# One of the modulation chunks leaves the attention loop of a one-core diffusion step and is weighed by VectorE during the output projection

## The chip, the cores and the metric

The kernel runs on one core of one Trainium2 chip. The metric is the device time of one launch in microseconds; lower is better. All data is float32 except a few small routing tables.

## What is computed

Two layers of a diffusion backbone over 384 tokens (128 context, 256 latent) of width 1024. Layer 0 mixes by a short convolution and an eight-head latent attention, layer 1 by a chunked gMLP. Each layer then runs a mixture of 16 experts. Every mixer and every mixture is shifted, scaled and gated by six vectors of 1024 that come from the condition:

```python
    for l in range(DEPTH):
        mp = jnp.split((jax.nn.silu(c_ctx) @ w_ada[l] + b_ada[l])[None, None, :], 6, axis=-1)
        ms = jnp.split((jax.nn.silu(c) @ w_ada[l] + b_ada[l])[:, None, :], 6, axis=-1)
        hp = modulate(rmsnorm(xp, g_mix[l]), mp[0], mp[1])
        hs = modulate(rmsnorm(xs, g_mix[l]), ms[0], ms[1])
        ...
        xp = xp + mp[2] * op
        xs = xs + ms[2] * os_
        hp = modulate(rmsnorm(xp, g_ffn[l]), mp[3], mp[4])
        hs = modulate(rmsnorm(xs, g_ffn[l]), ms[3], ms[4])
        xp = xp + mp[5] * moe(hp, router_w, router_b, moe_w1[l], moe_w3[l], moe_w2[l])
        xs = xs + ms[5] * moe(hs, router_w, router_b, moe_w1[l], moe_w3[l], moe_w2[l])
```

The change is about one product of this kind, `silu(c) @ w_ada`.

## The kernel before

**The modulation chunks.** The product with `w_ada` (1024 x 12288 over both layers) is cut into 16 chunks "ada 0" to "ada 15" of 768 columns and 3 MB each; four chunks make the vectors of one half-layer. A chunk goes through four steps. `ada_rows(n)` on TensorE multiplies the weights by the two condition vectors: 48 matmuls of 128 columns, which the trace counts as 96 records. ScalarE copies the result to `ada_row`. `ada_turned(n)` on TensorE transposes it. `ada(n)` on VectorE adds the bias into `mod` in three instructions; for every n with n % 4 == 2 a fourth computes `gain1`.

Two chunks, `WEIGHED = (3, 4)`, are done another way. VectorE multiplies each of the eight 128x768 weight tiles by the condition values and adds them up, once for each of the two condition vectors (`weigh`, 16 instructions). TensorE then only sums over the partitions (`weighed_rows`, 12 short matmuls with a 0/1 matrix `pick`).

**The weight ring.** Weights are streamed through six slots of 3 MB: four in `ring`, one in `work`, one in `state`. `CHUNKS` is the order of all loads, `homes()` deals slots to them. SyncE (SP) issues the loads strictly in the order written, and waits ahead of each until the chunk that held the slot has been used (`wait_used`). An expert's 3 MB come as two loads.

**The attention loop.** After the projections TensorE runs ten steps, s = 0 to 9. Step s holds `score(s)`, the ada work that `attention_ada(s)` gives to it (one `ada_rows` and one `ada_turned` in most steps), `turn(s - 1)` (seven transposes of the softmax output of head s - 1), and in odd steps from 3 on `attend`, the product with the values for two heads. VectorE takes the maxima of head s (`maxima`), ScalarE the exponentials (`exps`), and VectorE in the next step divides by the sums (`normalise`). In step s VectorE first copies the second half of the transposes of head s - 2, then normalises head s - 1, then takes the maxima of head s, then adds the bias of an ada chunk. From head 2 on, its copy waits for the `attend` of the pair before.

**From the attention to the experts of layer 0.** `mix_out(0)` on TensorE makes eight output tiles of 64 matmuls in all; VectorE adds each one to the residual `xT` (two instructions), and sums up squares that ScalarE makes. `norm(1)` needs all squares. `dispatch(0)` does ada 11, the router, the transposes of the tokens (`h_row`), which ScalarE stores to `h_all` in DRAM, and the places of the tokens. GpSimd then gathers 128 tokens at a time by indirect DMA, and TensorE runs nine passes over 128 places each through the experts (`turn_h`, `up`, `down`). Layer 1 has the same dispatch and passes.

**PSUM.** All products share eight banks in turn, in the order of `PRODUCTS`. `opened` waits until the product eight places ahead has been taken.

Of the kernel before, what the change touches and what calls it, by code (L numbers as in the profile page):

```python
# [54 lines left out]
EARLY = 2  # L55
WEIGHED = (3, 4)
HALF_TILES = 3 * KD
# [45 lines left out]
def attention_ada(s):  # L103

    return [s + 4] if 1 <= s <= 6 else [], [s + 3] if 2 <= s <= 7 else []

# [4 lines left out]
def dispatch_products(l):  # L111
    return ([("ada_row", HEAD_ADA[l]), ("router", l), ("logits", l)] + [("h_row", l, t, c) for t in range(NT) for c in range(2)]
            + [("ada_t", HEAD_ADA[l]), ("slots", l), ("table", l, 0)])

# [11 lines left out]
       + ([("attend", s // 2 - 1)] if s >= 3 and s % 2 else [])]  # L126
    + [("mix_out", 0, d) for d in range(KD)] + [("norm", 1)]
    + dispatch_products(0)
# [68 lines left out]
def build(nc, a, out):  # L197
    ctx = ExitStack()
    with ctx:
# [69 lines left out]

        at[0] = KD * T  # L270
        v_rows = carve(NT, D)
        uT = carve(KD, T)
# [124 lines left out]
        def wait(eng, s, value):  # L397

            if not (isinstance(value, int) and value <= 0):
                eng.wait_ge(s, value)  # L400

        block = ctx.enter_context(nc.Block())


        @block.sync
        def _(sp):
# [64 lines left out]
            def load_experts(l):  # L471

                for j in (0, 1):
                    load_first(l, j)
# [5 lines left out]
                load("ada", HEAD_ADA[l])  # L480
                for j in (2, 3, 4):
                    load_first(l, j)
# [76 lines left out]
        def _(act):  # L559
# [13 lines left out]
            def take(ins, *key):  # L573
                ins.then_inc(taken[bank_of(key)[0]], 1)
# [180 lines left out]
            def dispatch(l):  # L755

                take(act.activation(logit_t[:, :], product("router", l)[:, 0:T], ACT.Identity), "router", l)
                ada(HEAD_ADA[l])
                wait_taken("logits", l)
                act.activation(s_score[:, :], s_score[:, :], ACT.Exp, scale=-1.0).then_inc(s_rexp, 1)  # L760
                for t in range(NT):
                    for c in range(2):
                        key = ("h_row", l, t, c)
                        take(act.activation(h_rows[:, t, c * 512:c * 512 + 512], product(*key)[:, :], ACT.Identity), *key)
                    for c in range(2):
                        wait_taken("h_row", l, t, c)
                    act.dma_start(h_all[t * P:t * P + P, :], h_rows[:, t, :]).then_inc(s_hstored, 16)
# [55 lines left out]
        def _(dve):  # L823
# [121 lines left out]
            def weigh(n, tiles):  # L945

                i, (s, turn) = WEIGHED.index(n), HOME["ada", n]
                w = ring[:, s, :].rearrange("p (k n) -> p k n", n=ADA_COLS)
                if 0 in tiles:
# [87 lines left out]

            def mix_out(l):
                for d in range(KD):
                    residual(l, 0, d, product("mix_out", l, d))  # L1040
                    if d >= 2:
                        add_square(2 * l + 1, d - 1)
                add_square(2 * l + 1, KD - 1)

# [101 lines left out]
            def place(l):  # L1146
# [12 lines left out]
                step(cube[0])  # L1159
                step(dve.tensor_reduce(s_own[:, :].rearrange("p (t j) -> p t j", t=NT), cube[1], AX.X, ALU.add))  # L1160
                ada(HEAD_ADA[l])

# [163 lines left out]
        def _(pe):  # L1326
# [24 lines left out]
            def weighed_rows(n):  # L1351

                pe.wait_ge(s_weighed, 2 * KD * (WEIGHED.index(n) + 1))
                pe.wait_ge(s_pick, 3)
                ps = opened("ada_row", n)
# [227 lines left out]
            mix_out(0)  # L1583


            def dispatch(l):
# [13 lines left out]
                for t in range(NT):  # L1600
                    for c in range(2):
                        ps = opened("h_row", l, t, c)
                        for k in range(4):
                            mm = pe.transpose(ps[:, k * P:k * P + P], hT[:, 4 * c + k, t * P:t * P + P], ident[:, :])
                        closed(mm, "h_row", l, t, c)
                ada_turned(HEAD_ADA[l])
                pe.wait_ge(s_mask, l + 1)
# [288 lines left out]
```

## Time and profile before

| | |
|---|---|
| median of 3 runs | 748.4 us (747.16 to 751.85) |
| the profiled execution: time, span | 752.46 us, 750.4 us |
| TensorE matmul busy | 672.7 us, 90% |
| VectorE busy | 258.2 us, 34% |
| ScalarE busy | 159.1 us, 21% |
| mean granted TensorE clock | 0.954 |

The profiled execution took 2.1 us more than its span, and 4.1 us more than the median. Busy times of the engines overlap. The granted clock is given as a share of full speed, 2.4 GHz; the other level is 1.2 GHz, shown as 0.50.

### The profile page before, as it was taken

How to read it: one execution, taken by the hardware profiler on the slowest of the kernel's cores; microseconds unless marked ns; L12 is line 12 of the kernel's file. 1: busy time of each engine (PE TensorE's matmuls, PEld its weight loads, DVE VectorE, ACT ScalarE, POOL GpSimd, SP SyncE). 2: the span in 40 equal slices, each digit the busy share in tenths (PEclk: the TensorE clock that was granted, in tenths of full speed). 3: DMA queues.
4: the chain of work that ended last, by engine and by line, in shares of the span. 5: the costliest groups of instructions: out<-in, count | busy, mean ns of one | idle time of the engine just before them, and what ended most of it. 6: DMA issues, size and time to landing. Idle time of an engine off the chain costs nothing.

```text
span 750.4 us, 11306 instructions
## 1 busy us (share of the span) xinstructions
PE 672.7 (90%) x4744; PEld 345.0 (46%) x4744; DVE 258.2 (34%) x600; ACT 159.1 (21%) x316; POOL 32.5 (4%) x88
## 2 busy tenths in 40 slices
PE   4699999999989858999977799999998499999884
PEld 2555555557755523333323545556654333333242
DVE  0504678366511473121101620020425711211027
ACT  2301000253411231111111430131013311111023
POOL 2000000000000011000002000000000010010020
PEclk9999999999999987999999999999999889999898
DMA  9996030769974378899997895423745778999852
GB/s 368 381 425 273 33 140 1 317 274 424 424 307 167 131 298 299 324 401 418 425 428 283 324 397 227 183 111 121 314 169 217 290 299 309 405 424 424 352 197 84
DMA packets 27556, 213.63 MB, mean 285 GB/s; under 512 B 2768, under 2 KB 6640, under 8 KB 15856
## 3 DMA queue, kind: packets, MB, share of 16 engines
q1 hardware_dynamic: 17568, 182.06, 59.7%
q0 software_dynamic: 4320, 15.73, 6.0%
q10 hardware_dynamic: 5616, 15.09, 5.1%
q8 instruction: 39, 0.64, 0.3%
q14 instruction: 13, 0.11, 0.0%
HBM read 199.62 MB, written 13.25 MB: 284 GB/s over the span
## 4 chain that ended last, share of the span: by engine, by line
PE 77%; DVE 9%; DMA 8%; issue 2%; ACT 2%; POOL 1%; SPq 0%; POOLq 0%; DVEq 0%; ACTq 0%
PE bank L1447 29%; PE bank L1691 17%; PE bank L1706 8%; PE bank L1784 6%; DMA ring<-in_ada_w 3%; PE bank L1381 2%; DVE work L844 2%; PE bank L1500 2%; DMA state<-y_slots,index 2%; PE bank L1593 2%; DVE xT L847 2%; DMA work<-h_all,table 2%; DVE state L888 1%; PE bank L1672 1%; PE bank L1392 1%
## 5 line engine op out<-in xcount | busy, mean ns | idle before, releaser
L1447 PE MATMUL bank<-state,ring 128*128 128x384 f32 x416 | 136.1, 487 | 1.2 <-ACT state L614 1.2
L1691 PE MATMUL bank<-ring,work 128*32 128x512 f32 x896 | 110.2, 636 | 7.4 <-issue 7.4
L1447 PEld LDWEIGHTS bank<-state,ring 128*128 128x128 f32 x416 | 78.3, 190 | 54.9 <-issue 2.1
L1447 PE MATMUL bank<-work,ring 128*128 128x384 f32 x256 | 83.8, 489 | 0.3 <-DVE work L844 0.3
L1447 PEld LDWEIGHTS bank<-work,ring 128*128 128x128 f32 x256 | 48.6, 191 | 35.1 <-DVE work L844 1.3
L1691 PEld LDWEIGHTS bank<-ring,work 128*32 128x32 f32 x896 | 28.8, 116 | 73.6 <-issue 73.5
L1706 PE MATMUL bank<-ring,work 128*32 128x512 f32 x448 | 50.9, 595 | 2.6 <-ACT work L734 2.6
L1244 DVE COPY work<-bank 128x512 f32<-128x512 f32 x18 | 12.4, 691 | 111.6 <-PE bank L1676 111.6
L847 DVE SCALAR_TENSOR_TENSOR xT<-bank,mod,xT 128x128 f32<-128x128 f32 x64 | 22.5, 411 | 68.4 <-PE bank L1447 67.2
L1784 PE MATMUL bank<-ring,state 128*128 128x512 f32 x96 | 43.3, 612 | 2.4 <-ACT state L614 2.4
L536 POOL DMA_INDIRECT work<-h_all,table x18 | 17.1, 951 | 591.0 <-DMA h_all<-work 455.1
L596 ACT ACTIVATE state<-xT 128x384 f32<-128x384 f32 x40 | 20.6, 522 | 99.2 <-DVE xT L847 88.1
L1418 PE MATMUL bank<-state,share 128*128 128x384 f32 x58 | 22.6, 548 | 10.3 <-ACT state L596 10.3
L1784 PEld LDWEIGHTS bank<-ring,state 128*128 128x128 f32 x96 | 18.7, 196 | 25.7 <-issue 25.2
L1268 DVE COPY work<-bank 128x512 f32<-128x512 f32 x18 | 12.4, 692 | 50.4 <-PE bank L1706 50.4
L1691 PE MATMUL bank<-work 128*32 128x512 f32 x160 | 28.9, 594 | 0.0
L1691 PE MATMUL bank<-state,work 128*32 128x512 f32 x96 | 28.9, 594 | 0.0
L1706 PEld LDWEIGHTS bank<-ring,work 128*32 128x32 f32 x448 | 13.3, 109 | 31.0 <-issue 28.0
L847 DVE SCALAR_TENSOR_TENSOR work<-ring,csil,work 128x768 f32<-128x768 f32 x28 | 26.3, 1011 | 0.0
L1381 PE MATMUL bank<-ring,csil 128*32 128x128 f32 x704 | 22.3, 280 | 4.1 <-DMA ring<-in_ada_w 4.1
L844 DVE TENSOR_TENSOR mod<-bank,smalls 128x8 f32<-128x8 f32 (+1 forms) x32 | 3.8, 158 | 63.3 <-PE bank L1400 63.1
L1672 PE MATMUL bank<-smalls,work 128*128 128x128 f32 x72 | 12.7, 302 | 14.2 <-DMA work<-h_all,table 7.7
(211 smaller groups left out, 724.1 us busy)
## 6 DMA issues: line engine op xcount, KB each, us to landing
ring<-in_moe SPq DMA_DIRECT2D x24, 2048.0 KB, 10.0
ring<-in_ada_w SPq DMA_DIRECT2D x12, 3072.0 KB, 15.1
ring<-in_moe SPq DMA_DIRECT2D x24, 1024.0 KB, 17.9
work<-in_ada_w SPq DMA_DIRECT2D x3, 3072.0 KB, 10.1
work<-in_moe SPq DMA_DIRECT2D x4, 2048.0 KB, 11.6
state<-in_moe SPq DMA_DIRECT2D x4, 2048.0 KB, 14.5
y_slots<-work ACTq DMA_DIRECT2D x16, 512.0 KB, 9.8
ring<-in_gm_in SPq DMA_DIRECT2D x4, 2048.0 KB, 9.0
```

The lines of the kernel that those rows point to most:

```text
L536: pool.indirect_dma_start(h_slot[:, p % 2, :], None, h_all, bass.IndirectOffsetOnAxis(ap=table[:, l, p:p + 1], axis=0))\
L596: act.activation(sq[:, k % 4, :], xT[:, k, :], ACT.Square).then_inc(s_sq, 1)
L844: return dve.tensor_tensor(o, x, y, op)
L847: return dve.scalar_tensor_tensor(out=o, in0=x, scalar=s, in1=y, op0=op0, op1=op1)
L1381: mm = pe.matmul(ps[32 * g:32 * g + 32, 0:P], csil[:, k, :], w[:, k, g * P:g * P + P], start=(k == 0), stop=(k == KD - 1))
L1418: mm = pe.matmul(ps[:, 0:T], share[:, n, :], sq[:, sq_at[0] % 4, :], start=(k == 0), stop=(k == tiles - 1))
L1447: mm = pe.matmul(ps[:, 0:T], w[:, k, j * P:j * P + P], x[:, k, :], start=(k == 0), stop=(k == KD - 1))
L1500: mm = pe.matmul(ps[:, 0:T], w_q[:, k, h * P:h * P + P], q_a[:, k, :], start=(k == 0), stop=(k == NQ - 1))
L1672: tr = pe.transpose(bank[2][:, k * P:k * P + P], h_slot[:, b, k * P:k * P + P], ident[:, :])
L1691: mm = pe.matmul(bank[p % 2][rows, :], h_slotT[:, p % 2, k * P + BLOCK * n:k * P + BLOCK * n + BLOCK], held(place_of(e))[:, k * 512:k * 51 ...
L1706: mm = pe.matmul(bank[4 + half][rows, :], hiddenT[:, p % 2, c * P + BLOCK * n:c * P + BLOCK * n + BLOCK], held(place_of(e))[:, at_:at_ + 5 ...
L1784: mm = pe.matmul(ps[:, :], hT[:, k, t * P:t * P + P], w[:, k, :], start=(k == 0), stop=(k == KD - 1))
```

## The change

Ada 10 (the third chunk of the modulation of the gMLP in layer 1) becomes the third weighed chunk. It leaves steps 6 and 7 of the attention loop. VectorE weighs its tiles 0 and 1 before the first residual of `mix_out(0)`, and two more tiles after each of the first three residuals, into `mid_weighed`, a place in `work` that the attention has left free. TensorE's `ada_rows(10)` then stands behind `mix_out(0)`, and the copy, the transposes and the bias of ada 10 stand in `dispatch(0)` ahead of those of ada 11. The slot of ada 10 goes to expert 1 of layer 0, as before. SP now issues the load of ada 11 ahead of expert 1, whose load waits until the weighing is over. The slots of all chunks are as before. The banks of the products between the steps 6 and the router shift by one or two.

```diff
-WEIGHED = (3, 4)
+WEIGHED = (3, 4, 10)
...
 def attention_ada(s):
 
-    return [s + 4] if 1 <= s <= 6 else [], [s + 3] if 2 <= s <= 7 else []
+    return [s + 4] if 1 <= s <= 5 else [], [s + 3] if 2 <= s <= 6 else []
...
-            + [("ada_t", HEAD_ADA[l]), ("slots", l), ("table", l, 0)])
+            + [("ada_t", n) for n in ((10, 11), (15,))[l]] + [("slots", l), ("table", l, 0)])
...
-    + [("mix_out", 0, d) for d in range(KD)] + [("norm", 1)]
+    + [("mix_out", 0, d) for d in range(KD)] + [("ada_row", 10), ("norm", 1)]
...
+        at[0] = KD * T
+        mid_weighed = carve(2, ADA_COLS)
+        mid_pick = carve(2, 32)
...
             def load_experts(l):
 
-                for j in (0, 1):
+                for j in range(1 if l == 0 else 2):
                     load_first(l, j)
...
                 load("ada", HEAD_ADA[l])
-                for j in (2, 3, 4):
+                for j in range(1 if l == 0 else 2, SLOTS + 1):
                     load_first(l, j)
...
             def mix_out(l):
+                if l == 0:
+                    product("attend", HEADS // 2 - 1)
+                    step(dve.memset(mid_pick[:, :, :], 0.0))
+                    for side in range(2):
+                        dve.memset(mid_pick[:, side, side:side + 1], 1.0).then_inc(s_pick, 1)
+                    weigh(10, (0, 1))
                 for d in range(KD):
                     residual(l, 0, d, product("mix_out", l, d))
                     if d >= 2:
                         add_square(2 * l + 1, d - 1)
+                    if l == 0 and d < 3:
+                        weigh(10, (2 * d + 2, 2 * d + 3))
                 add_square(2 * l + 1, KD - 1)
...
             mix_out(0)
-
+            ada_rows(10)
```

In `dispatch(0)`, `ada(10)` now stands ahead of `ada(11)` on ScalarE and on VectorE, and `ada_turned(10)` ahead of `ada_turned(11)` on TensorE.

TensorE in steps 6 and 7 of the attention loop. L1519 to L1523 are `score`, L1381 and L1392 `ada_rows`, L1400 `ada_turned`, L1534 `turn`. Before:

```order
L1519 MATMUL bank<-work,state 128x128
L1520 MATMUL bank<-work,state 128x384
L1523 MATMUL bank<-work,state 128x384
L1381 MATMUL bank<-ring,csil 32x128 x32
L1392 MATMUL bank<-ring,csil 32x128 x16
L1400 MATMUL bank<-smalls,ada_row 128x128 x2
L1534 MATMUL bank<-smalls,work 128x128 x7
L1519 MATMUL bank<-work,state 128x128
L1520 MATMUL bank<-work,state 128x384
L1523 MATMUL bank<-work,state 128x384
L1400 MATMUL bank<-smalls,ada_row 128x128 x2
L1534 MATMUL bank<-smalls,work 128x128 x7
```

The same two steps after, where the line numbers are 22 higher:

```order
L1541 MATMUL bank<-work,state 128x128
L1542 MATMUL bank<-work,state 128x384
L1545 MATMUL bank<-work,state 128x384
L1422 MATMUL bank<-smalls,ada_row 128x128 x2
L1556 MATMUL bank<-smalls,work 128x128 x7
L1541 MATMUL bank<-work,state 128x128
L1542 MATMUL bank<-work,state 128x384
L1545 MATMUL bank<-work,state 128x384
L1556 MATMUL bank<-smalls,work 128x128 x7
```

The 48 matmuls of ada 10 are gone from step 6 and its transposes from step 7; the transposes of ada 9 stay in step 6.

VectorE at the start of `mix_out(0)`. Before, the residual additions (L847) follow the last copy of the attention (L1023):

```order
L1023 COPY work<-bank 128x384
L847 SCALAR_TENSOR_TENSOR xT<-bank,mod,xT 128x128
L847 SCALAR_TENSOR_TENSOR xT<-bank,mod,xT 128x256
L847 SCALAR_TENSOR_TENSOR xT<-bank,mod,xT 128x128
L847 SCALAR_TENSOR_TENSOR xT<-bank,mod,xT 128x256
```

After, where L1034 is that copy and L857 both the residuals and the weighing:

```order
L1034 COPY work<-bank 128x384
L1052 MEMSET work 128x64
L1054 MEMSET work 128x1 x2
L972 TENSOR_SCALAR work<-ring,csil 128x768 x2
L857 SCALAR_TENSOR_TENSOR work<-ring,csil,work 128x768 x2
L857 SCALAR_TENSOR_TENSOR xT<-bank,mod,xT 128x128
L857 SCALAR_TENSOR_TENSOR xT<-bank,mod,xT 128x256
L857 SCALAR_TENSOR_TENSOR work<-ring,csil,work 128x768 x4
L857 SCALAR_TENSOR_TENSOR xT<-bank,mod,xT 128x128
L857 SCALAR_TENSOR_TENSOR xT<-bank,mod,xT 128x256
```

Four weighing instructions stand ahead of the first residual, and four more behind each of the first three.

VectorE at the end of `place(0)` in the dispatch, between the two products with `s_move` and the choice of the later places. After:

```order
L1179 TENSOR_REDUCE work<-work 128x33
L854 TENSOR_TENSOR mod<-bank,smalls 128x8
L854 TENSOR_TENSOR mod<-bank,smalls 128x4
L854 TENSOR_TENSOR mod<-bank,mod 128x4
L857 SCALAR_TENSOR_TENSOR gain<-mod,smalls 128x16
L854 TENSOR_TENSOR mod<-bank,smalls 128x8
L854 TENSOR_TENSOR mod<-bank,smalls 128x4
L854 TENSOR_TENSOR mod<-bank,mod 128x4
L854 TENSOR_TENSOR work<-smalls,s_tmp 128x3x96
```

Before, only the three instructions of ada 11 stand there; the four ahead of them, with the gain, are new at this place.

## Rows read from the trace of the kernel before

**Rows 1.** The page, part 4: the chain that ended last, by engine.
```profile
PE 77%; DVE 9%; DMA 8%; issue 2%; ACT 2%; POOL 1%; SPq 0%; POOLq 0%; DVEq 0%; ACTq 0%
```

**Rows 2.** Timeline of TensorE, steps 6 to 9: start, duration, instructions, idle time before.
```profile
198.35 1.95 PE L1381 MATMUL bank<-ring,csil 128*32 128x128 f32 x64
...
201.10 0.44 PE L1400 MATMUL bank<-smalls,ada_row 128*128 128x128 f32 x2
201.38 0.93 PE L1534 MATMUL bank<-smalls,work 128*128 128x128 f32 x7
...
203.66 0.38 PE L1400 MATMUL bank<-smalls,ada_row 128*128 128x128 f32 x2
204.12 0.98 PE L1534 MATMUL bank<-smalls,work 128*128 128x128 f32 x7
205.03 1.73 PE L1549 MATMUL bank<-work 128*64 128x128 f32 x16
208.54 0.98 PE L1534 MATMUL bank<-smalls,work 128*128 128x128 f32 x7 [1.78 <-DVE work L1015]
210.45 2.93 PE L1549 MATMUL bank<-work 128*64 128x128 f32 x16 [0.92 <-DVE work L1023]
```

**Rows 3.** Timeline of VectorE in the same steps.
```profile
197.48 0.95 DVE L1015 TENSOR_SCALAR work<-work,sm_inv 128x128 f32<-128x128 f32 x3
...
202.92 0.17 DVE L1013 RECIPROCAL sm_inv<-sm_sum 128x3 f32<-128x3 f32 x1
203.12 0.95 DVE L1015 TENSOR_SCALAR work<-work,sm_inv 128x128 f32<-128x128 f32 x3
...
205.30 0.23 DVE L844 TENSOR_TENSOR mod<-bank,smalls 128x8 f32<-128x8 f32 x2
...
205.77 0.17 DVE L847 SCALAR_TENSOR_TENSOR gain<-mod,smalls 128x16 f32<-128x16 f32 x1
206.87 0.56 DVE L1023 COPY work<-bank 128x384 f32<-128x384 f32 x1 [0.93 <-PE bank L1549]
...
207.54 0.94 DVE L1015 TENSOR_SCALAR work<-work,sm_inv 128x128 f32<-128x128 f32 x3
```

**Rows 4.** Timeline of ScalarE: the last record of the exponentials of head 6.
```profile
201.36 0.21 ACT L682 ACTIVATION_READ_ACCUMULATOR work<-bank,sm_neg 128x1 f32 x1
```

**Rows 5.** Timeline of VectorE: the first two residuals of mix_out(0).
```profile
219.22 0.74 DVE L847 SCALAR_TENSOR_TENSOR xT<-bank,mod,xT 128x128 f32<-128x128 f32 x2 [9.03 <-PE bank L1447]
224.38 0.74 DVE L847 SCALAR_TENSOR_TENSOR xT<-bank,mod,xT 128x128 f32<-128x128 f32 x2 [4.42 <-PE bank L1447]
```

**Rows 6.** Groups by form, VectorE, 90 to 122 us: count, busy us, mean ns, idle before.
```profile
L847 DVE SCALAR_TENSOR_TENSOR work<-ring,csil,work 128x768 f32<-128x768 f32 x22 | 20.7, 1010 | 0.0
...
L961 DVE TENSOR_SCALAR work<-ring,csil 128x768 f32<-128x768 f32 x2 | 1.1, 616 | 0.2 <-PE bank L1362 0.2
```

**Rows 7.** Timeline of SP's queue: the loads of expert 1 and of expert 2.
```profile
201.23 0.33 SPq L459 DMA_DIRECT2D ring<-in_moe  x1
...
234.69 0.33 SPq L459 DMA_DIRECT2D ring<-in_moe  x1
```

**Rows 8.** Windows: each engine's busy time, then granted clock, DMA share, GB/s.
```profile
210.00:215.00 5.00, 4.55 (x20) 2.77 (x21) 0.19 (x1) 0.49 (x1) 0.00 (x0) 0.66 0.83 290
...
245.00:250.00 5.00, 5.00 (x17) 2.88 (x17) 1.21 (x3) 0.52 (x1) 0.00 (x0) 1.00 0.00 0
```

**Rows 9.** Groups by form, TensorE, 90 to 122 us: the sum over partitions of a weighed chunk.
```profile
L1358 PE MATMUL bank<-work 128*32 128x128 f32 x16 | 0.6, 279 | 0.0
```

**Rows 10.** Timeline of TensorE, layer 0: the norm, pass 0's up, the second gather.
```profile
257.28 0.91 PE L1430 MATMUL bank<-state,share 128*128 128x384 f32 x2 [1.98 <-DVE state L844]
...
286.25 5.14 PE L1691 MATMUL bank<-ring,work 128*32 128x512 f32 x32
292.15 0.66 PE L1672 MATMUL bank<-smalls,work 128*128 128x128 f32 x4 [0.76 <-DMA work<-h_all,table]
```

**Rows 11.** Timeline of TensorE, layer 1: the same 32 records of pass 0.
```profile
601.33 6.32 PE L1691 MATMUL bank<-ring,work 128*32 128x512 f32 x32
```

More of the change, by code:

```diff
@@ L400, in wait, with weighed_of @@
                 eng.wait_ge(s, value)
+        def weighed_of(n):
+            return (weighed, pick) if n < 10 else (mid_weighed, mid_pick)
         block = ctx.enter_context(nc.Block())
@@ L757, in dispatch @@
                 take(act.activation(logit_t[:, :], product("router", l)[:, 0:T], ACT.Identity), "router", l)
+                if l == 0:
+                    ada(10)
                 ada(HEAD_ADA[l])
@@ L947, in weigh @@
                 i, (s, turn) = WEIGHED.index(n), HOME["ada", n]
+                weighed = weighed_of(n)[0]
                 w = ring[:, s, :].rearrange("p (k n) -> p k n", n=ADA_COLS)
@@ L1038, in mix_out @@
             def mix_out(l):
+                if l == 0:
+                    product("attend", HEADS // 2 - 1)
[3 more added lines that the diff above has]
+                    weigh(10, (0, 1))
                 for d in range(KD):
@@ L1160, in place @@
                 step(dve.tensor_reduce(s_own[:, :].rearrange("p (t j) -> p t j", t=NT), cube[1], AX.X, ALU.add))
+                if l == 0:
+                    ada(10)
                 ada(HEAD_ADA[l])
@@ L1351, in weighed_rows @@
             def weighed_rows(n):
+                weighed, pick = weighed_of(n)
                 pe.wait_ge(s_weighed, 2 * KD * (WEIGHED.index(n) + 1))
-                pe.wait_ge(s_pick, 3)
+                pe.wait_ge(s_pick, 3 if n < 10 else 5)
                 ps = opened("ada_row", n)
@@ L1605, in dispatch @@
                         closed(mm, "h_row", l, t, c)
+                if l == 0:
+                    ada_turned(10)
                 ada_turned(HEAD_ADA[l])
```

## The prediction, made before the changed kernel ran

> **What bounds the kernel now.** I began with the chain that ended last: 77% of it is TensorE, 9% VectorE, 8% DMA [rows 1]. So work taken from TensorE counts, if TensorE is not made to wait in its place. Next came TensorE's timeline over the last steps of the attention loop, since that is where work is taken out. The reader should look there for two things: where a start follows the end before it, and where a bracket shows a wait. Up to step 7 TensorE goes from one thing to the next without a marked wait; the first are 1.78 us ahead of the transposes of head 7, for VectorE's normalise, and 0.92 us ahead of the last attend [rows 2]. Then VectorE and ScalarE in the same steps, to see how far ahead of TensorE they are [rows 3, 4]. Last, the places to which the work moves: the gaps of VectorE in mix_out, and the covers of the dispatch.
>
> **Part 1: the attention loop (a gain).** What leaves TensorE is ada_rows(10), from 198.35 to 201.10, 2.75 us, and the transposes of ada 10, worth 0.28 us when nothing waits (201.10 to 201.38 for those of ada 9) [rows 2]. That is 3.03 us of work. How much of it shortens the loop depends on the softmax of heads 6 and 7, so I replay the steps.
>
> Score(6) ends at about 198.4 as before. The transposes of ada 9 follow (0.28), and turn(5) can begin at 198.70: the normalised head 5 was there at 197.48 + 0.95 = 198.43 [rows 2, 3]. Turn(5) and score(7) take 203.66 - 201.38 = 2.28 us [rows 2], so TensorE is done with them at 200.98. Now turn(6) needs normalise(6), which needs the exponentials of head 6. They depend on score(6), which has not moved, and end at 201.36 + 0.21 = 201.57 [rows 4]. Before, VectorE normalised head 6 only at 203.12, because its copy of head 5 stood ahead and waited for turn(5); now that copy is over in time. Normalise takes 0.20 us for the reciprocal (202.92 to 203.12) and 0.95 us for the products [rows 3]: it ends at about 202.7, where before it ended at 204.07. Turn(6) begins at about 202.75 in place of 204.12: 1.37 us earlier, with a new wait of 1.8 us ahead of it.
>
> From there everything keeps its distance: turn(6), attend(2) 0.91 us later, the copy that waits for attend(2), normalise(7), turn(7) [rows 2, 3]. The maxima and exponentials of head 7 move by the same 1.37 us, as the maxima follow normalise(6) on VectorE. Mix_out(0) begins 1.37 us earlier. The other 1.66 us of the 3.03 turn into TensorE's wait for the softmax. **Term: -1.4 us**, bounds -3.0 (all of the removed work) and 0 (all of it turns into waits).
>
> **Part 2: weighing in mix_out.** 14 instructions of the adding form and 2 of the multiplying form. Their spans overlap: 22 of them kept VectorE busy for 20.7 us, 0.94 each. I price them at their full 1.01 and 0.62 us [rows 6] as the upper bound: 15.4 us in all. Before the first residual stand 2 x 0.62 + 2 x 1.01 = 3.3 us and three small memsets; VectorE had been idle for 9.03 us there, of which 9 or so remain, since copy and residual move together [rows 5]. Then residuals come every 5.16 us, with 4.42 us idle between them [rows 5], and four weighing instructions take at most 4.04 us. Behind the third residual stands a sum of squares too, smaller than the residual's 0.74 us, which makes it 0.4 us too much at the most, and the later residuals have no weighing behind them, so nothing is left of it at the end. TensorE does not wait for these residuals: its banks are eight deep. **Term: 0.** If the cover were gone, each 1 us of overrun would delay the norm by 1 us.
>
> **Part 3: the second expert's load.** The wait for the weighing is a new one in SP's queue; queued behind it are experts 2, 3 and 4. It is over after the third residual, a sum of squares and four weighing instructions: 219.22 + 2 x 5.16 - 1.37 + 0.74 + at most 0.74 + 4.04 = 233.7. Expert 2 was issued at 234.69, and could be at 233.3 now [rows 7], so it loses some 1 us with the issuing of expert 1. The 3 MB of expert 2 had landed before 245, as the DMA engines then stood at 0 GB/s from 245 to 250 [rows 7, 8]; that is at most 10.3 us for 3 MB. Two of them from 233.7 on are there by 254.3 at the latest, about when the eighth tile of mix_out ends and frees expert 3's slot (219.22 + 7 x 5.16 - 1.37 = 254.0). Expert 1 is first used at 286 [rows 10]. What expert 1 did at 201.23 [rows 7] hid nothing. **Term: 0**, with over 30 us of cover.
>
> **Part 4: behind mix_out and in the dispatch.** The 12 short matmuls of the weighed chunk (24 records) cost about 0.9 us (16 of the records took 0.6) [rows 9] and lie in the 1.98 us in which TensorE waits for the last squares [rows 10]. Term 0; without the cover, 0.9. ScalarE's copy (0.3 us) and the two transposes (0.3 us) lie ahead of waits for VectorE's routing. VectorE's four instructions of ada 10 do cost: from 205.30 to 205.94, 0.64 us [rows 3], and they stand ahead of the choice of the later places, for which pass 0's up waits on TensorE. So up begins 0.64 us later relative to the rest, and then TensorE waits 0.76 us for the second gather by DMA anyway [rows 10]. The cover is just enough: **term 0**, bounds 0 and +1.2, the latter because the same 32 records took 6.32 us in layer 1 and 5.14 here [rows 10, 11].
>
> **The sum.** -1.4 us. The profiled execution, 752.46 us, would take 751.1. The runs' median is 748.4, 4.1 us less than that execution, and I apply the term to it: **747.0 us**.
>
> **The clock.** The trace shows the granted clock at 0.66 for 210 to 215 us [rows 8]. The drop follows the two waits of 1.78 and 0.92 us, and the last attend took 2.93 us where the one before took 1.73 [rows 2]. After the change there is a third wait of 1.8 us, 2.6 us ahead of these. The Trainium skill, "TensorE: Matmul & The Clock Gate", section "HAM oscillation — how this bites in real kernels", names idle gaps longer than these as what brings the clock down; by it the added wait would cost nothing and the sum would stay -1.4. The trace does not agree with it, since gaps of 1.78 and 0.92 us had a drop behind them. The same page says that the moment of switching is not tied to the start of the kernel, so it may fall otherwise from one execution to the next; one trace can't show that.
>
> **Rivals.**
> - *All the removed work is gained*: -3.0 us, 745.4 us. For it: no marked wait in steps 6 and 7. Against it: the replay finds head 6's softmax in the way, from rows whose causes have not moved.
> - *Nothing is gained* (the filler was free): 748.4 us. It takes the replay to be off by 1.4 us, or up(0) at the duration of layer 1 to eat the gain (0.64 + 1.18 - 0.76 = 1.1 us late).
> - *Slower, by the clock*: with three waits in the last steps the drop comes one attend earlier. Attend(2) then takes 2.93 - 1.73 = 1.2 us more, and the seven transposes of head 7 up to twice their 0.98 us, 0.9 more. Against -1.4 this gives +0.7: 749.1 us. It decides when the clock falls before about 204.5. For it: the drop after short waits. Against it: no wait of 1.8 us alone, with full work on both sides, has a drop behind it in these rows.
> - *The weighing is late*: if the 16 instructions took over 5 us more than priced, the residuals and the norm would follow, at 1 us each. Nothing in the rows supports a weighing at over 1.01 us each.
>
> **How the numbers follow.** The forecast of -1.4 (from -2 to -0.7) has 0.55. The full gain has 0.15, nothing 0.13, the clock 0.13, a late weighing or another loss 0.04. The range takes in the full gain with a scatter of about 1 us below it, 744.3, and the clock's case with about 1.5 us above it, 750.6; the runs before already lie from 747.16 to 751.85. A change of under 1% (7.5 us) can hardly be told from none, and no case reaches it: within 1% 0.95, faster 0.03, slower 0.02.
>
> **What the changed profile would show.** In step 6 turn(5) some 0.3 us behind score(6), then a wait of 1.5 to 2 us ahead of turn(6) for normalise; attend(2) over 1.7 us, not 2.9; the start of mix_out(0) near 212.0. Weighing in all the gaps of the first four residuals, the residuals still 5.16 us apart. Expert 1 issued near 233.7, expert 2 right behind it. The 12 matmuls ahead of the norm's, with a wait of about 1.2 us left. Pass 0's up in the dispatch about 0.6 us later relative to the router, and almost no wait ahead of the second gather's transposes. The prediction is wrong if the loop's end moves by more than 2 us or not at all, or if a wait for a load shows up in the expert passes.

## The result, and the profile after

| | before | changed |
|---|---|---|
| median of 20 runs each | 747.7 us (744.73 to 751.85) | 750.57 us (744.67 to 753.97) |
| ratio to before | | 1.0033, interval 1.0016 to 1.0049 |
| the profiled execution: time, span | 752.46 us, 750.4 us | 751.93 us, 750.1 us |
| mean granted TensorE clock of the timed runs | 0.9568 (35 runs, those beside the first experiments) | 0.9545 (20 runs) |

The change is slower by 2.5 us (1.2 to 3.7). Here and below, a difference in us with a range is worked out from the ratio and its interval. A ratio is an estimate from the single runs, not the quotient of the two medians, and the two differ by up to 0.16%. The prediction was 1.4 us faster, 747.0 us. The measured median lies just inside the range (744.3 to 750.6), and the difference is within 1%, which had 0.95; but the direction is wrong, and the interval excludes the forecast term.

The chain that ended last, by engine, for the changed kernel (for [rows 1]):

```profile
PE 77%; DVE 10%; DMA 6%; issue 3%; ACT 2%; POOL 1%; SPq 0%; POOLq 0%; DVEq 0%; ACTq 0%
```

It is the same but for 2 points of share that moved from DMA to VectorE and issue. The answer lies in the timeline of TensorE in the changed kernel, steps 6 to 9, the norm and the dispatch (for [rows 2, 10]):

```profile
198.51 0.38 PE L1422 MATMUL bank<-smalls,ada_row 128*128 128x128 f32 x2
198.74 0.98 PE L1556 MATMUL bank<-smalls,work 128*128 128x128 f32 x7
...
203.06 1.52 PE L1556 MATMUL bank<-smalls,work 128*128 128x128 f32 x7 [1.82 <-DVE work L1026]
204.51 2.82 PE L1571 MATMUL bank<-work 128*64 128x128 f32 x16
209.06 0.98 PE L1556 MATMUL bank<-smalls,work 128*128 128x128 f32 x7 [1.73 <-DVE work L1026]
210.97 3.25 PE L1571 MATMUL bank<-work 128*64 128x128 f32 x16 [0.92 <-DVE work L1034]
214.15 42.94 PE L1469 MATMUL bank<-work,ring 128*128 128x384 f32 x128
257.02 0.64 PE L1380 MATMUL bank<-work 128*32 128x128 f32 x16
257.48 0.40 PE L1384 MATMUL bank<-work 128*32 128x128 f32 x8
259.07 0.91 PE L1452 MATMUL bank<-state,share 128*128 128x384 f32 x2 [1.19 <-DVE state L854]
...
264.67 5.86 PE L1615 MATMUL bank<-state,smalls 128*32 128x384 f32 x16 [1.93 <-DVE state L907]
...
288.78 5.26 PE L1715 MATMUL bank<-ring,work 128*32 128x512 f32 x32
293.97 0.66 PE L1696 MATMUL bank<-smalls,work 128*128 128x128 f32 x4
```

Turn(5) follows score(6) at once, and the new wait of 1.82 us stands ahead of turn(6), as predicted. But turn(6) then takes 1.52 us where it took 0.98, and attend(2) 2.82 where it took 1.73 [rows 2]. The windows of the same trace show the granted clock, the third number from the end of each line (before it stand each engine's busy time and instructions, behind it the DMA share and GB/s):

```profile
200.00:203.00 3.00, 1.24 (x4) 0.38 (x2) 2.15 (x10) 2.45 (x8) 0.00 (x0) 1.00 0.97 415
203.00:207.00 4.00, 3.94 (x23) 2.72 (x23) 1.30 (x5) 1.58 (x6) 0.00 (x0) 0.57 0.55 229
207.00:210.00 3.00, 1.27 (x11) 0.74 (x7) 1.58 (x5) 1.17 (x3) 0.00 (x0) 1.00 0.00 0
210.00:217.00 7.00, 6.08 (x22) 3.44 (x22) 3.18 (x8) 0.90 (x2) 0.00 (x0) 0.51 0.28 80
```

It fell right behind the new wait (0.57 from 203 to 207, mostly the 1.2 GHz level), came back (1.00 from 207 to 210), and fell again behind the two old waits (0.51 from 210 to 217, where before showed 0.66 from 210 to 215 [rows 8]). Mix_out(0) starts at 214.15, not at 212.0.

The weighing and the loads went as predicted. VectorE in the changed kernel: the softmax of head 6, then the first, second and fourth residual (for [rows 3, 5]):

```profile
201.85 0.17 DVE L1024 RECIPROCAL sm_inv<-sm_sum 128x3 f32<-128x3 f32 x1 [0.72 <-ACT work L690]
202.06 0.94 DVE L1026 TENSOR_SCALAR work<-work,sm_inv 128x128 f32<-128x128 f32 x3
...
221.01 0.74 DVE L857 SCALAR_TENSOR_TENSOR xT<-bank,mod,xT 128x128 f32<-128x128 f32 x2 [3.44 <-PE bank L1469]
221.67 3.79 DVE L857 SCALAR_TENSOR_TENSOR work<-ring,csil,work 128x768 f32<-128x768 f32 x4
...
226.17 0.74 DVE L857 SCALAR_TENSOR_TENSOR xT<-bank,mod,xT 128x128 f32<-128x128 f32 x2 [0.71 <-PE bank L1469]
...
236.49 0.74 DVE L857 SCALAR_TENSOR_TENSOR xT<-bank,mod,xT 128x128 f32<-128x128 f32 x2 [0.24 <-PE bank L1469]
```

The residuals stay 5.16 us apart (226.17 - 221.01), and 0.24 us of idle time is left ahead of the tightest. SP's queue in the changed kernel, experts 1 and 2 (for [rows 7]):

```profile
236.28 0.33 SPq L467 DMA_DIRECT2D ring<-in_moe  x1
237.12 0.43 SPq L467 DMA_DIRECT2D ring<-in_moe  x1
```

That is 236.28 where 233.7 was forecast, of which 214.15 - 212.0 = 2.15 us is the late start of mix_out(0). No matmul of layer 0's expert passes waited for a weight load, in this trace or in any other.

### The profile page after: what moved, and what is told of

It is laid out like the page before. It is cut to its first block, busy times and chain, and to the rows that moved or that the text cites. A ratio compares the mean times of both kernels' runs of the same rounds, so it can differ in the third digit from the quotient of the medians.

```text
span 750.1 us, 11182 instructions
## 1 busy us (share of the span) xinstructions
PE 669.8 (89%) x4672; PEld 343.6 (46%) x4672; DVE 272.5 (36%) x619; ACT 159.0 (21%) x316; POOL 32.6 (4%) x88
## 4 chain that ended last, share of the span: by engine, by line
PE 77%; DVE 10%; DMA 6%; issue 3%; ACT 2%; POOL 1%; SPq 0%; POOLq 0%; DVEq 0%; ACTq 0%
PE bank L1469 29%; PE bank L1715 18%; PE bank L1730 8%; PE bank L1808 6%; DVE work L854 3%; DMA ring<-in_ada_w 3%; PE bank L1403 2%; PE bank L1522 2%; DMA state<-y_slots,index 2%; PE bank L1615 2%; DVE xT L857 2%; DVE state L898 1%; PE bank L1571 1%; PE bank L1696 1%; DMA y_slots<-work 1%
## 5 line engine op out<-in xcount | busy, mean ns | idle before, releaser
L1715 PE MATMUL bank<-ring,work 128*32 128x512 f32 x896 | 108.2, 626 | 7.7 <-issue 7.7
L1730 PE MATMUL bank<-ring,work 128*32 128x512 f32 x448 | 50.9, 595 | 2.6 <-ACT work L742 2.6
L857 DVE SCALAR_TENSOR_TENSOR xT<-bank,mod,xT 128x128 f32<-128x128 f32 x64 | 22.5, 411 | 51.7 <-PE bank L1469 50.5
L857 DVE SCALAR_TENSOR_TENSOR work<-ring,csil,work 128x768 f32<-128x768 f32 x42 | 39.7, 1008 | 0.0
L898 DVE RECIPROCAL state<-state 128x384 f32<-128x384 f32 x6 | 15.3, 2551 | 28.6 <-ACT state L612 28.6
## 6 DMA issues: line engine op xcount, KB each, us to landing
ring<-in_ada_w SPq DMA_DIRECT2D x12, 3072.0 KB, 15.1
```

The source lines that it names most:

```text
L857: return dve.scalar_tensor_tensor(out=o, in0=x, scalar=s, in1=y, op0=op0, op1=op1)
L898: step(dve.reciprocal(rms, rms))
L1715: mm = pe.matmul(bank[p % 2][rows, :], h_slotT[:, p % 2, k * P + BLOCK * n:k * P + BLOCK * n + BLOCK], held(place_of(e))[:, k * 512:k * 51 ...
L1730: mm = pe.matmul(bank[4 + half][rows, :], hiddenT[:, p % 2, c * P + BLOCK * n:c * P + BLOCK * n + BLOCK], held(place_of(e))[:, at_:at_ + 5 ...
```

## The experiments

Four lengths are read from every trace. Attend(2) is the attend of heads 4 and 5, "the last attend" that of heads 6 and 7. **Loop**: from the start of the attend of heads 2 and 3 to the start of mix_out(0), which holds the whole edit. **Loop + mix_out**: the same, to the end of mix_out(0). **D1**: from the start of the router to pass 0's up in `dispatch(0)`. **D2**: from the same start to the second gather's transposes. In the changed kernel D1 is 288.78 - 264.67 = 24.11 us and D2 is 293.97 - 264.67 = 29.30. "Slow attends" counts which of the last two attends ran at the lower clock (2.8 to 3.3 us and not 1.73).

| trace | new wait | loop | slow attends | loop + mix_out | D1 | D2 |
|---|---|---|---|---|---|---|
| before | no | 18.34 | last | 60.33 | 23.37 | 29.27 |
| before_again | no | 17.14 | none | 58.69 | 23.54 | 28.69 |
| row_kept | no | 17.09 | none | 58.64 | 24.05 | 30.49 |
| row_kept_bias_early | no | 18.61 | last | 60.23 | 23.61 | 30.07 |
| changed | yes | 18.92 | both | 61.86 | 24.11 | 29.30 |
| changed_again_1 | yes | 17.30 | last | 58.85 | 24.10 | 30.27 |
| changed_again_2 | yes | 18.10 | both | 60.22 | 24.05 | 30.54 |
| bias_early | yes | 17.23 | last | 58.97 | 23.47 | 28.36 |
| without_ada10 | yes | 15.78 | none | 57.33 | 23.35 | 28.58 |
| without_again | yes | 18.19 | both | 60.25 | 23.38 | 28.50 |
| before_filled | filled | 17.14 | none | 58.69 | 23.41 | 29.63 |
| fill_step7 | filled | 16.42 | none | 57.96 | 24.02 | 30.08 |
| fill_steps789 | filled | 16.41 | none | 57.95 | 24.21 | 30.23 |
| fill_step7_free | filled | 15.78 | none | 57.33 | 24.23 | 30.24 |
| bias_early_filled | filled | 16.42 | none | 57.97 | 23.40 | 29.37 |
| both_repairs_free | filled | 15.78 | none | 57.33 | 23.62 | 30.07 |

"Filled" means that matmuls nobody uses stand where TensorE would wait, 24 in the new wait; before_filled, without the new wait, has 24 and 12 at the two old waits.

### Work in the waits: fill_step7, fill_steps789, before_filled

The edit of fill_step7, against the changed kernel. The products go to a bank that turn(6) overwrites:

```diff
+            def filler(key, count):
+
+                ps = opened(*key)
+                for i in range(count):
+                    g = i % 4
+                    pe.matmul(ps[32 * g:32 * g + 32, 0:P], csil[:, i % KD, :], ident[:, :], start=True, stop=True)
...
+                if s in {7: 24}:
+                    filler(("probs_t", s - 1, 0), {7: 24}[s])
                 if 1 <= s <= HEADS:
                     turn(s - 1)
```

> The changed kernel with 24 short matmuls (128 columns, condition vectors times the identity, into the bank of the next transposes, which overwrite them) put on TensorE in step 7 of the attention loop, ahead of the transposes of head 6, where the changed kernel waits 1.8 us for the softmax. They should take about 1.4 us, so nothing becomes later by work alone. Theory 'clock' (the new wait in step 7 brings the drop of TensorE's clock one attend earlier and so costs about 3 us more than the 1.4 us gained): the drop goes back to where it was, attend of heads 4 and 5 takes 1.7 us instead of 2.8, and the time is 0 to 2 us below the kernel before. Rival 'moved work' (the cost lies in mix_out and in the dispatch): no change against the changed kernel, about 2.5 us above the kernel before.

Fill_steps789 has the same, and 24 more in step 8 and 12 ahead of the last attend, that is, in all three waits:

> The changed kernel with such matmuls in all three waits at the end of the attention loop: 24 ahead of the transposes of head 6, 24 ahead of those of head 7, 12 ahead of the last attend. Theory 'clock': no drop at all up to mix_out, the last attend takes 1.7 us and mix_out(0) about 41.3 us; 2 to 4 us below the kernel before. Rival 'moved work': about 2.5 us above the kernel before, as the changed kernel.

Before_filled is the kernel before with the fillers of the two old waits alone:

> The kernel before, with 24 such matmuls ahead of the transposes of head 7 and 12 ahead of the last attend, the two places where it waits (1.78 and 0.92 us). Theory 'clock': its own drop at the end of the attention goes too, 1 to 2.5 us below the kernel before. Rival 'moved work': the same time as before, within 0.5 us.

Measured against before (747.99 us, 35 runs): fill_step7 748.56 us, ratio 1.0003 (0.9979 to 1.0027); fill_steps789 747.69 us, 0.9996 (0.9972 to 1.0021); before_filled 747.89 us, 1.0006 (0.9983 to 1.0028). TensorE in fill_step7:

```profile
202.91 1.52 PE L1553 MATMUL bank<-smalls,csil 128*32 128x128 f32 x48 [1.01 <-ACT work L704]
204.36 0.99 PE L1563 MATMUL bank<-smalls,work 128*128 128x128 f32 x7
205.28 1.73 PE L1578 MATMUL bank<-work 128*64 128x128 f32 x16
```

With 1.52 us of work in the wait, attend(2) is back at 1.73 us, and so is the last attend, whose two waits are still there. One trace would not decide it, as the drops vary from one execution to the next. The table does: some attend is slow in 5 of 6 traces with the new wait open and in none of 5 with it filled. So it is the gap that brought the clock down. The filler did cost something itself: it waited 1.01 us for its bank and ended 0.6 us late, which is the 16.42 against 15.78 of the table. The two old waits alone are worth little in the median: before_filled gains nothing that can be told, with an interval from -1.3 to +2.1 us.

Against the expectations: fill_step7 gave back what theory 'clock' said of the attends, and its +0.2 us (-1.6 to +2.0) is far from the +2.5 us of the rival. Fill_steps789 (-0.3 us, -2.1 to +1.6) missed the 2 to 4 us that theory 'clock' expected, and before_filled missed its 1 to 2.5 us.

### The removed matmuls put back: row_kept

The changed kernel, with the 48 matmuls of ada 10 in step 6 again, their result unused:

```diff
                     score(s)
+                if s == 6:
+                    w = weights(("ada", 10), ADA_COLS)
+                    ps = opened("ada_t", 9)
+                    for k in range(KD):
+                        for g in range(4):
+                            pe.matmul(ps[32 * g:32 * g + 32, 0:P], csil[:, k, :], w[:, k, g * P:g * P + P],
+                                      start=(k == 0), stop=(k == KD - 1))
+                    ada_ends(ps[:, P:2 * P], w)
                 ada(attention_ada(s)[1], attention_ada(s)[0])
```

> The changed kernel with the 48 matmuls of ada 10 put back on TensorE in step 6 as well (their result is not used), so that the attention loop is as before but for the two transposes, while the weighing in mix_out, the later load of expert 1 and the longer dispatch stay. Theory 'clock': within 1 us of the kernel before. Rival 'moved work': 2.5 to 4 us above the kernel before, since the 1.4 us gained in the loop are given back on top.

749.74 us against 747.99, ratio 1.0029 (1.0009 to 1.0050). That is +2.2 us (0.7 to 3.7), outside the 1 us of theory 'clock' and a little under the 2.5 of its rival: neither was right alone. In its one trace the loop is the one of before (17.09 us), with no slow attend, and yet the kernel is about as slow as the changed one. Hence the loop as a whole, gain and clock together, is worth little between the two, and the loss must stand elsewhere too. The two places that are left are the weighing with the loads, and the dispatch.

### The gain without the weighing: without_ada10

The kernel before, minus ada 10: its matmuls, transposes, copy and bias are left out, and zeros stand in for those modulation vectors of layer 1. Expert 1's load is held back until the slot has been filled by ada 10 and score(6) has run.

```diff
-    return [s + 4] if 1 <= s <= 6 else [], [s + 3] if 2 <= s <= 7 else []
+    return [s + 4] if 1 <= s <= 5 else [], [s + 3] if 2 <= s <= 6 else []
...
+            pool.memset(mod[:, 2, 12:18, :], 0.0)
...
                 ada(*attention_ada(s)[1])
+                if s == 6:
+                    modulation_ready(2)
```

> The kernel before with ada 10 left out of the attention loop and done nowhere (its part of the modulation of layer 1 is zero; its 3 MB are still loaded), so that the loop alone changes: no weighing, no other order of loads, no longer dispatch. Theory 'clock': the loop gains 1.4 us of work time and loses about as much or more by an additional stretch at the lower clock, 0 to 1.5 us above the kernel before. Rival 'moved work' (the loop's gain is real, and what is added behind it eats it): 1.4 us or more below the kernel before.

751.05 us against 749.33 (35 runs of before beside it), ratio 1.0024 (1.0000 to 1.0047). 3.03 us of TensorE's work and 0.64 us of VectorE's are gone, only one memset on GpSimd is added, and the kernel is not faster: +1.8 us (0 to 3.5), which rules out the 1.4 us of gain. Its mean granted clock is 0.952 where before had 0.956. This is the plainest evidence that removing the work is itself no gain. One trace of it has the loop at 15.78 us, 1.36 us under the 17.14 of before_again, so the gain is there when the clock holds. The zeros also change which tokens go where in layer 1. Its traces give no sign that this costs time: from the second gather to the sum of the experts' outputs layer 1 took 111.7 us in both, where the other fourteen took 111.4 to 115.0.

### The place of the bias: bias_early, row_kept_bias_early, bias_early_filled

The changed kernel, with the copy, the transposes and the bias of ada 10 moved from the dispatch into the waits ahead of the router:

```diff
+    return ([("ada_row", HEAD_ADA[l])] + [("ada_t", 10)] * (l == 0) + [("router", l), ("logits", l)]
...
                 load_exp()
+                ada(10)
                 modulate(1)
...
             def dispatch(l):
+                if l == 0:
+                    ada(10)
                 route(l)
...
                 ada_rows(HEAD_ADA[l])
+                if l == 0:
+                    ada_turned(10)
                 ps = opened("router", l)
```

> The changed kernel with copy, transposes and bias of ada 10 moved out of the critical part of the dispatch: the copy right behind the table load of the norm, the transposes behind the row matmuls of ada 11, VectorE's four instructions ahead of the router's work, where VectorE waits 2 us for the logits. From the router's first matmul to pass 0's up the changed kernel took 24.11 us, the one before 23.37; this should give 23.4 again. Theory 'moved work': most of the loss is here, so the time falls to the kernel before or below. Theory 'clock': it gains 0.7 us at most against the changed kernel and stays 1.5 to 2 us above the kernel before.

Row_kept_bias_early joins this edit with the one of row_kept:

> The kernel row_kept (the changed kernel with the 48 matmuls of ada 10 put back into step 6 on TensorE) with the bias of ada 10 early as in bias_early. What is left of the change is the weighing in mix_out, the 12 short matmuls behind it and the later load of expert 1. If row_kept's 0.29% are the dispatch, this is within 0.5 us of the kernel before. If the weighing or the load costs time by itself, it stays about 1.5 us above.

Bias_early_filled joins it with the fillers of fill_steps789:

> The changed kernel with both repairs: the filling matmuls in the three waits at the end of the attention loop and the bias of ada 10 early. If the two causes add, this is 1.4 us of loop time, some 0.5 us of clock and 0 us of dispatch below the kernel before: 1 to 3 us below it.

Against 749.33 us: bias_early 750.57 us, 1.0002 (0.9970 to 1.0035); row_kept_bias_early 748.6 us, 1.0006 (0.9983 to 1.0030); bias_early_filled 746.92 us, 0.9977 (0.9954 to 0.9999). Bias_early is thus +0.15 us (-2.2 to +2.6), less than the 1.5 to 2 us that theory 'clock' expected. Row_kept_bias_early, +0.4 us (-1.3 to +2.2), holds the weighing, the 12 short matmuls and the later load of expert 1 and is within its 0.5 us: these cost nothing that can be told, and of the two places left by row_kept the dispatch remains. Bias_early_filled, -1.7 us (-3.4 to -0.1), is within its 1 to 3 us. TensorE in bias_early, router, pass 0's up, second gather:

```profile
261.67 5.86 PE L1617 MATMUL bank<-state,smalls 128*32 128x384 f32 x16 [1.56 <-DVE state L907]
...
285.14 4.96 PE L1715 MATMUL bank<-ring,work 128*32 128x512 f32 x32
290.03 0.66 PE L1696 MATMUL bank<-smalls,work 128*128 128x128 f32 x4
```

D1 is 285.14 - 261.67 = 23.47 us, as before. In the table D1 is 24.02 to 24.23 us in all seven traces with the late bias and 23.35 to 23.62 in the nine others: +0.65 us or so, as VectorE's 0.64 us said. D2 is 30.16 us in the mean with the late bias (29.30 to 30.54) and 29.17 in the others (28.36 to 30.07), +1.0, with more scatter. From the router to the end of moe_add(0), the sum of the experts' outputs, the means are 159.5 us (159.0 to 159.9) and 158.7 (157.6 to 159.5): 0.85 us are left at the end of the layer. So nothing covered it. Why not shows in before_again, TensorE, the same place:

```profile
285.63 5.22 PE L1691 MATMUL bank<-ring,work 128*32 128x512 f32 x32
290.78 0.66 PE L1672 MATMUL bank<-smalls,work 128*128 128x128 f32 x4
```

The transposes follow the up with no wait for the gather; the 0.76 us of [rows 10] are missing. The windows of the ada 11 stretch, before first, then before_again, show what differed:

```profile
259.00:263.00 4.00, 3.74 (x78) 3.48 (x70) 3.96 (x5) 2.22 (x4) 0.00 (x0) 0.62 0.94 399
```

```profile
259.00:263.00 4.00, 2.06 (x47) 1.16 (x38) 3.97 (x7) 1.91 (x5) 0.00 (x0) 1.00 0.97 410
```

GpSimd in the same two traces, the first of the gathers, in the same order:

```profile
279.17 1.08 POOL L536 DMA_INDIRECT work<-h_all,table  x1 [274.44 <-DMA h_all<-work]
```

```profile
277.22 1.14 POOL L536 DMA_INDIRECT work<-h_all,table  x1 [272.49 <-DMA h_all<-work]
```

In the trace that the prediction had, the clock was down there (0.62), and this gather was issued 279.17 - 262.88 = 16.29 us behind the router's start, in before_again 15.13. The other traces divide in the same way. Three of sixteen (before, without_again, before_filled) have a stretch at the lower clock within 4.3 us of the router's start. In these three the gather was issued at 16.25 to 16.31 us, and the second one landed at 28.5 to 29.6. In the thirteen others it was issued at 15.1 to 15.65 us and the second one landed at 21.5 to 22.6, long before TensorE asked for it. So the cover of Part 4 belonged to some executions, not to the kernel.

D2 scatters for another reason. In all sixteen traces the clock is at the lower level behind the waits of the dispatch, and it comes back 26.2 to 30.0 us behind the router's start. Where it came back at 26.2 us D2 is 28.36, where it came back at 30.0 it is 30.54. How much of the +1.0 us of D2 is the bias and how much is this clock, the traces do not tell; the 0.65 us of D1 lie ahead of it.

### The same kernels again: changed_again_1, changed_again_2, before_again, without_again

No edit; one execution each, to see whether the drops stand where they stood.

> The changed kernel once more, for a second trace. Theory 'clock': a stretch at the lower clock begins between 200 and 212 us again, and attend of heads 4 and 5 or of heads 6 and 7 (or both) takes over 2.5 us and not 1.7; mix_out(0) begins near 214 where such a stretch is, and near 211.9 where there is none.

> The changed kernel, a third trace, with the same expectation as for the second. If two of the three traces show no stretch at the lower clock ahead of mix_out(0), the theory 'clock' has too little to stand on.

> The kernel before, for a second trace. Its two waits (1.78 and 0.92 us) brought a drop in the first trace. Theory 'clock' expects it less often than in the changed kernel: with it mix_out(0) begins near 213.3, without it near 212.1.

> The kernel without_ada10 once more. Its first trace had no drop in the loop (mix_out(0) began at 210.80), though its runs spent more time at the lower clock than the kernel before did (mean granted clock 0.952 against 0.956). Theory 'clock': this trace, or else most of its runs, has a stretch at the lower clock between 199 and 212 us, and mix_out(0) then begins 1 us or more later than 210.80.

751.17, 753.48, 745.93 and 750.71 us, one run each, beside a run of before of 751.71: single times that decide nothing. The traces say more. The expected drops are there: a slow attend in both traces of the changed kernel and in without_again, none in before_again. Only the start of mix_out(0), 212.55 and 212.93 us in the two changed traces, is not near 214, as the drops cost less there than in the first one. TensorE in changed_again_2:

```profile
202.67 0.98 PE L1556 MATMUL bank<-smalls,work 128*128 128x128 f32 x7 [1.82 <-DVE work L1026]
203.58 3.00 PE L1571 MATMUL bank<-work 128*64 128x128 f32 x16
```

In changed_again_1:

```profile
203.10 0.98 PE L1556 MATMUL bank<-smalls,work 128*128 128x128 f32 x7 [1.82 <-DVE work L1026]
204.01 1.73 PE L1571 MATMUL bank<-work 128*64 128x128 f32 x16
209.37 3.25 PE L1571 MATMUL bank<-work 128*64 128x128 f32 x16 [0.92 <-DVE work L1034]
```

In before_again:

```profile
209.38 0.98 PE L1534 MATMUL bank<-smalls,work 128*128 128x128 f32 x7 [1.78 <-DVE work L1015]
211.29 1.74 PE L1549 MATMUL bank<-work 128*64 128x128 f32 x16 [0.92 <-DVE work L1023]
```

The same wait of 1.82 us is followed by 3.00 us for attend(2) in one execution and by 1.73 in the next, and the two old waits by 2.93 [rows 2] or 1.74. The waits are fixed, the drop is not. Over the table, with the new wait attend(2) is slow in 3 traces of 6 and the last attend in 5 of 6; without it 0 and 2 of 4; with fillers neither in 6 of 6.

### A filler that costs nothing: fill_step7_free, both_repairs_free

Fill_step7_free takes a bank for the filler that is free already:

```diff
-                    filler(("probs_t", s - 1, 0), {7: 24}[s])
+                    filler(("probs_t", 7, 0), {7: 24}[s])
```

> The kernel fill_step7 with its 24 filling matmuls going to the bank of the first transposes of head 7, which is free when they are issued, so that they start at once. If the loop's gain of 1.4 us is real wherever the clock stays up, the loop from the attend of heads 2 and 3 to mix_out(0) takes 15.8 us where no drop lies in it (fill_step7 had 16.42), and the time is about 0.6 us below fill_step7. If the softmax were the bound anyway, the loop would stay at 16.4.

Both_repairs_free is bias_early_filled with that bank for its first two fillers:

> The kernel bias_early_filled (filling in three waits, bias of ada 10 early) with the first filling in the free bank. Loop of 15.8 us in place of 16.42; 2 to 3 us below the kernel before. If it is no better than bias_early_filled (0.23% below), the 0.6 us are lost in the scatter.

Against 748.87 us (23 runs): fill_step7_free 748.7 us, 0.9991 (0.9964 to 1.0017), with the loop at 15.78 us as expected; both_repairs_free **745.79 us, 0.9951 (0.9931 to 0.9972)**, 3.7 us (2.1 to 5.2) faster than before, where 2 to 3 were expected, with a mean granted clock of 0.960 against 0.955. TensorE in both_repairs_free:

```profile
201.33 1.52 PE L1553 MATMUL bank<-smalls,csil 128*32 128x128 f32 x48
203.22 0.98 PE L1563 MATMUL bank<-smalls,work 128*128 128x128 f32 x7 [0.37 <-DVE work L1026]
...
208.50 0.86 PE L1553 MATMUL bank<-smalls,csil 128*32 128x128 f32 x24
209.49 1.73 PE L1578 MATMUL bank<-work 128*64 128x128 f32 x16
```

The filler runs from 201.33, the wait behind it is 0.37 us, no attend is slow, and the loop is 15.78 us: the whole predicted gain.

## Why the prediction was wrong, point by point

**Part 1, the work: right.** The wait ahead of turn(6) is 1.82 us (forecast 1.8), and where the clock holds the loop is 17.14 - 15.78 = 1.36 us shorter (forecast 1.37). That the other 1.66 us would turn into a wait was right too.

**Part 1, "From there everything keeps its distance": the step that failed.** It holds in work, not in time, because the new wait brings the clock down. Take per trace the excess of loop + mix_out over the shortest one of its kind. With the new wait it is 4.53, 1.52, 2.89, 1.64, 0 and 2.92 us over 57.33, mean 2.25; without it 1.64, 0, 0 and 1.54 over 58.69, mean 0.8. So the clock takes 1.45 us more with the wait than without it, and the work taken out gives 1.36: the term is not -1.4 but +0.1 us. That difference of means has a standard error of about 0.8 us, so its size is loose. Its sign rests on more: without_ada10 is not faster, and slow attends stand in 5 of 6 traces with the wait open and in none of 5 with fillers in it. The ratios agree: filling took 0.3 to 0.4% off the changed kernel (1.0033 to 1.0003 and 0.9991) and 0.25 to 0.5% off bias_early (1.0002 to 0.9977 and 0.9951).

**Parts 2 and 3, and the short matmuls of Part 4: right.** The sum over the partitions took 0.64 us and 0.40 us in two overlapping groups, 257.02 to 257.88, and left 1.19 us of the norm's wait, as forecast. The weighing and the later load cost nothing that can be told (row_kept_bias_early), and no matmul waited for a load.

**Part 4, "The cover is just enough: term 0": mis-sized.** It is +0.65 us in D1, +0.85 at the end of the layer and about +1.0 in D2, inside the bounds of 0 to +1.2. The cover was read from one trace in which the clock was down ahead of it. Moving the bias ahead of the router gives D1 back. By the ratios to the before of the same set that is worth 0.31, 0.23 and 0.19% (changed to bias_early, row_kept to row_kept_bias_early, fill_steps789 to bias_early_filled), that is 1.4 to 2.3 us. None of the three is clear of noise by itself, and the medians can't be compared across the sets, as those of before alone go from 747.7 to 749.33 us.

**The clock.** The prediction had the mechanism as a rival and gave it 0.13 and +0.7 us. Its case against ("no wait of 1.8 us alone, with full work on both sides, has a drop behind it in these rows") was an argument from the absence of such a wait in before: there was none to look at. The place was right, ahead of 204.5, and attend(2) took 2.82 us where 2.93 was priced. The slow transposes were those of head 6 (1.52 us), not of head 7, which stayed at 0.98. What it did not see is that the old drop can grow: in the changed trace the last attend takes 3.25 us (2.93 before), the clock is still at 0.51 up to 217 us, and mix_out takes 42.94 where it took 41.99. Nor did it see that the drop comes in some executions only.

The Trainium skill, "TensorE: Matmul & The Clock Gate", section "HAM oscillation — how this bites in real kernels", names longer idle gaps as the cause; by it the wait costs nothing. The measurements decide against that here: a slow attend in 5 of 6 traces with gaps of 1.82 us and less.

**The sum, and what stays open.** Loop +0.1 and dispatch +0.65 to +1.0 make +0.8 to +1.1 us, where 2.5 (1.2 to 3.7) were measured. Some 1.5 us (between 0.1 and 2.9) have no place yet. The mean granted clock can't settle it. From 0.9568 to 0.9545 is 0.0023 x 2 x 748 = 3.4 us more at the lower level, and over the 35 runs of before such a microsecond goes with about 0.3 us of time, which makes 1.0 us. But before had 0.9556 and 0.9552 in two other sets, which is more than half of that difference. The three changed traces against the two of before give more, +0.8 for loop and mix_out and 30.04 - 28.98 = +1.06 for D2, 1.9 together, but that is a mean over few traces whose drops move. Row_kept (+2.2) and without_ada10 (+1.8) have such a remainder as well, and both_repairs_free is 3.7 us faster where the loop and D2 explain 1 to 2. The kernels with a remainder are also those whose mean clock is below that of before, and the two fastest have the highest clock.

A later drop is a likely place for a part of it. In every trace TensorE waits 2.37 us ahead of the gMLP of layer 1. Before, then before_again:

```profile
431.90 22.54 PE L1784 MATMUL bank<-ring,state 128*128 128x512 f32 x48 [2.37 <-ACT state L614]
...
572.07 1.12 PE L1430 MATMUL bank<-state,share 128*128 128x384 f32 x2 [1.98 <-DVE state L844]
```

```profile
430.18 20.84 PE L1784 MATMUL bank<-ring,state 128*128 128x512 f32 x48 [2.37 <-ACT state L614]
...
568.65 1.58 PE L1430 MATMUL bank<-state,share 128*128 128x384 f32 x2 [1.98 <-DVE state L844]
```

From the first of these starts to the second it is 140.17 us in before and 138.47 in before_again. The sixteen traces fall into two kinds: eight take 138.5 us, and eight take 140.1 to 140.2, 1.7 us more, with a stretch at the lower clock behind that wait. The longer kind stands in 6 of the 7 traces with a slow attend and in 2 of the 9 without one: in 5 of 6 with the new wait open, in 2 of 4 without it, in 1 of 6 with fillers. As an estimate from these counts, the new wait would cost 1.7 x (5/6 - 2/4) = 0.6 us more there. The counts are small and the place was picked after the traces were seen, so that the later drop follows on the earlier one is a lead and not shown. The rest of the 1.5 us stays open.

## What to carry to other kernels

Work that fills a wait of the engine in front may be worth its own time and more in clock: before taking some out of TensorE's stream, replay what wait it leaves, and put a price on the clock for each wait of 1 to 2 us that stands close to others. Where the wait can't be closed, matmuls into a bank that is free, ended before the real operand is there, kept the clock here; a bank that still has to be read makes the filler itself late. And a cover of under 1 us is to be read from more than one execution, since here a drop of the clock ahead of it made it, in 3 executions of 16.

## What was not expected of the hardware

A single wait of 1.82 us, with 2.6 us of matmuls behind it and TensorE busy throughout ahead of it (3.00 of 3.00 us from 198 to 201), had the halved clock right behind it in 3 executions of 6. With 1.52 us of small matmuls in it (24 of 128 columns) none of five traces had a drop there. In the changed trace the full clock came back by itself (0.57 from 203 to 207 us, 1.00 from 207 to 210) and fell again. Whether a drop follows a given wait is not fixed by the program: between three executions of the changed kernel the waits agreed to 0.01 us, and attend(2) took 2.82, 1.73 and 3.00 us.
